# Expert weights read as one 16 KB run per partition, with strided transposes to match

## The reference

```python
def _moe(h, w_router, router_bias, w_gate, w_up, w_down):
    hf = h.reshape(-1, shp[-1])
    combine = _route(hf, w_router, router_bias).astype(h.dtype)
    y = jnp.zeros_like(hf)
    for e in range(N_EXPERTS):
        a = jax.nn.silu(hf @ w_gate[e]) * (hf @ w_up[e])
        y = y + combine[:, e:e + 1] * (a @ w_down[e])
```

## Time and profile before

| | us |
|---|---|
| median of 3 runs | 1851.9 |
| profiled execution, its own time | 1853.53 |
| its span, first to last instruction | 1851.9 |
| mean granted TensorE clock (share of full) | 0.952 |
| PE busy | 1625.3 (88%) |
| DMA queue of SP: 160256 packets, 327.17 MB | 49.4% of 16 engines |
| DMA queue of POOL: 17136 packets, 66.13 MB | 9.5% of 16 engines |

### The profile page before, as it was taken

The page is one execution under the profiler, slowest core; times in us unless marked ns, Lnnn a source line. Parts: engine busy times, 40 slices in busy tenths (PEclk is TensorE's granted clock), DMA queues, the critical chain, the costliest instruction groups (busy, mean ns, idle before and its releaser), DMA issues. The chain is left out here.

```text
span 1851.9 us, 16016 instructions
## 1 busy us (share of the span) xinstructions
PE 1625.3 (88%) x6163; PEld 743.8 (40%) x6163; DVE 481.4 (26%) x1230; ACT 339.5 (18%) x759; POOL 131.6 (7%) x219
## 2 busy tenths in 40 slices
PE   4799998789999999699999969998899939987771
PEld 0244445554444445144444414445444424432220
DVE  1432027850011123301101155117501230011003
ACT  1011027760000021001110112027500111010000
POOL 0100000010000000300000020000200010001001
PEclk9899999999999998899999989999999959998886
DMA  9972232010303044999999996342333177999993
GB/s 345 384 244 91 46 126 119 22 51 32 131 6 136 0 149 160 388 394 365 388 393 393 391 378 206 93 136 97 99 118 113 48 293 273 326 369 387 377 393 110
DMA packets 178194, 396.74 MB, mean 214 GB/s; under 512 B 23694, under 2 KB 27822, under 8 KB 177928
## 3 DMA queue, kind: packets, MB, share of 16 engines
q1 hardware_dynamic: 160256, 327.17, 49.4%
q0 software_dynamic: 17136, 66.13, 9.5%
q10 hardware_dynamic: 724, 2.38, 0.3%
HBM read 373.27 MB, written 34.18 MB: 220 GB/s over the span
## 5 line engine op out<-in xcount | busy, mean ns | idle before, releaser
L1425 PE MATMUL bank<-ring_sb,HT_sb 128*128 128x512 f32 x672 | 296.0, 596 | 4.1 <-ACT HT_sb L703 1.5
L1490 PE MATMUL bank<-ring_sb,HT_sb 128*128 128x512 f32 x576 | 253.3, 592 | 1.4 <-ACT QR_sb L794 1.4
L1425 PEld LDWEIGHTS bank<-ring_sb,HT_sb 128*128 128x128 f32 x672 | 125.8, 191 | 151.2 <-issue 147.6
L1605 PE MATMUL bank<-ring_sb,QR_sb 128*64 128x512 f32 x608 | 148.2, 644 | 41.1 <-DMA ring_sb<-w_e_up 41.1
L1490 PEld LDWEIGHTS bank<-ring_sb,HT_sb 128*128 128x128 f32 x576 | 109.3, 190 | 138.7 <-issue 136.8
L1494 PE MATMUL bank<-ring_sb,QR_sb 128*128 128x512 f32 x288 | 129.5, 592 | 0.0
L1374 PE MATMUL bank<-ring_sb,cT_sb 128*2 128x512 f32 x384 | 95.9, 651 | 31.1 <-DMA ring_sb<-w_mod 30.3
L1591 PE MATMUL bank<-ring_sb,QR_sb 128*128 128x512 f32 x208 | 98.4, 629 | 3.4 <-ACT QR_sb L840 3.4
L1466 PE MATMUL bank<-WK_sb,KR_sb 128*64 128x128 f32 x960 | 68.3, 280 | 36.3 <-ACT WK_sb L804 35.5
L1605 PEld LDWEIGHTS bank<-ring_sb,QR_sb 128*64 128x64 f32 x608 | 49.2, 148 | 126.3 <-issue 126.2
L1621 PE MATMUL bank<-ring_sb,QR_sb 128*128 128x512 f32 x208 | 91.8, 594 | 0.0
(11 more groups left out here) (214 smaller groups left out, 1361.7 us busy)
## 6 DMA issues: line engine op xcount, KB each, us to landing
ring_sb<-w_e_gate SPq DMA_DIRECT2D x32, 2048.0 KB, 19.0
ring_sb<-w_e_up SPq DMA_DIRECT2D x32, 2048.0 KB, 21.4
ring_sb<-w_e_down SPq DMA_DIRECT2D x32, 2048.0 KB, 21.5
ring_sb<-w_mod SPq DMA_DIRECT2D x24, 2048.0 KB, 16.3
ring_sb<-w_in SPq DMA_DIRECT2D x22, 2048.0 KB, 17.3
MB_sb<-mod_d POOLq DMA_DIRECT2D x16, 512.0 KB, 8.7
ring_sb<-w_branch SPq DMA_DIRECT2D x8, 1024.0 KB, 10.0
ring_sb<-w_out SPq DMA_DIRECT2D x4, 2048.0 KB, 10.3
```

What stands on the lines that cost most here:

```text
L1425: ins = mm(bank[j % 4][:, :], HT[:, k, P * t:P * t + P], WR[slot][:, k], start=(k == 0), stop=(k == KD - 1))
L1490: ins = mm(bank[i % 2][:, :], HT[:, k, P * t:P * t + P], WR[wg][:, k], start=(k == 0), stop=(k == KD - 1))
L1605: ins = mm(bank[0][HALF * side:HALF * side + HALF, :], hgT[q % 2][:, k, 0:HALF], WR[slot][:, k], start=(k == 0), stop=(k == KD - 1))
```

## The change

The weight loads take a different row order: partition p now gets rows p*8 to p*8+7 of gate and up (p*4 to p*4+3 of down), which lie one after the other in DRAM, 16 KB for each partition. Before it got rows p, p + 128, p + 256, ..., in runs of 2 KB (gate, up) or 4 KB (down). Block k of the weights therefore holds the rows p*8 + k, so block k of the transposed rows must hold the channels p*8 + k: the transposes read their stationary operand with a step of 8 elements (rows) or 4 elements (hidden values). Neither the number of instructions nor their order changes, nor any wait. All other weights (`w_mod`, `w_in`, `w_branch`, `w_out`) keep their loads, and the rows, stores and gathers of POOL too. The last two hunks of the diff lie in a path that runs only when an expert gets more tokens than it has rows.

```diff
             def expert_source(l, e, j):
                 w = t_in[("w_e_gate", "w_e_up", "w_e_down")[j]]
                 w = w[l, e] if isinstance(e, int) else w[l, bass.ds(e, 1)].rearrange("o k n -> (o k) n")
-                return w.rearrange("(k p) n -> p k n", p=P)
+                return w.rearrange("(p k) n -> p k n", p=P)
...
-                def rows_of(src, q, dst, count):
-                    if full_rows(l, q):
-                        return transposes(src, dst, count)
+                def spread(src, rows, dst, count, first=0, parts=None):
+
+                    by_k = src.rearrange("q (p k) -> q k p", k=parts or count)
                     for k in range(count):
-                        ins = mm(dst[:, HALF * k:HALF * k + HALF], src[0:HALF, P * k:P * k + P],
-                                 ident[0:HALF, 0:HALF], start=True, stop=True, is_transpose=True)
+                        ins = mm(dst[:, rows * k:rows * k + rows], by_k[0:rows, first + k], ident[0:rows, 0:rows],
+                                 start=True, stop=True, is_transpose=True)
                     return ins
...
                     if full_rows(l, q):
                         for g in range(2):
-                            ins = transposes(hg[q % 2][:, CW * g:CW * g + CW], bank[6 + g], 4)
+                            ins = spread(hg[q % 2], P, bank[6 + g], 4, 4 * g, KD)
                     else:
-                        ins = rows_of(hg[q % 2], q, bank[6], KD)
+                        ins = spread(hg[q % 2], HALF, bank[6], KD)
                     ins.then_inc(hg_tr, 1)
...
-                    rows_of(ea, q, bank[2], 4).then_inc(ea_tr, 1)
+                    spread(ea, P if full_rows(l, q) else HALF, bank[2], 4).then_inc(ea_tr, 1)
```

More of the change, by code:

```diff
@@ L1664, in _ @@
                         for g in range(2):
-                            ins = transposes(hg[0][:, CW * g:CW * g + CW], bank[6 + g], 4)
+                            ins = spread(hg[0], P, bank[6 + g], 4, 4 * g, KD)
                         ins.then_inc(q["hg_tr"], 1)
@@ L1673, in _ @@
                         eng.wait_ge(q["a"], n + 1)
-                        transposes(ea, bank[3], 4).then_inc(q["a_tr"], 1)
+                        spread(ea, P, bank[3], 4).then_inc(q["a_tr"], 1)
                         eng.wait_ge(q["aT"], n + 1)
```

## The result

| | us |
|---|---|
| before, median of 6 runs | 1854.51 (1851.51 to 1856.8) |
| after, median of 6 runs | 1863.47 (1859.33 to 1867.74) |
| ratio | 1.005, 95% interval 1.0038 to 1.0063 |
| profiled execution of after, own time and span | 1859.33 and 1857.7 |

The change makes the kernel 0.5% slower, about 9 us (1863.47 less 1854.51). The profiled execution of after is the fastest of its six; its span is 5.8 us longer than that of before, and only these 5.8 us can be followed in the trace.

A forecast was written before the change was run, and what follows sets the result against it. PE was taken to bound layer 0, weight loads layer 1's last nine experts, with each stage's start a third place. -12.8 - 1.8 + 13.6 + 4.6 = +3.6 us on 1851.9 gave about 1855 us, range 1838 to 1869.

The forecast's parts named there:

- Gain in layer 1: Layer 1's last nine experts, bound by weight loads: faster long runs save 12.8 us (10 to 19).
- The start of layer 0: SP's 16 KB runs delay POOL's scatters and row load before layer 0's first transposes: +13.6 us (0 to +17).
- The rival without starving: Layer 0's start: scatters are not delayed by long runs, so the +13.6 falls away: 1842 us; chance 0.25.
- Eight periods: Layer 1's tail, 1656.81 to 1798.12 us: 1.22 us saved per expert, 9.8 us in all (8.8 to 13.6).
- Ahead of expert 7: Layer 1, loads queued before expert 7's 5.15 us wait: 2.3 us by run prices, 3 us taken.
- The waits and the stride in layer 0: Two 0.9 us weight waits vanish (-1.8); strided transposes cost 0.2 us an expert, +4.6 over 23 experts of both layers.
- Strided loads twice as long: Transposes of 23 experts: weight loads 140 ns longer each, up to 39 us, 1890 us at most; chance 0.17.
- one sign of being wrong: Expert transposes: taking 1.5 times as long would show the forecast wrong.
- The end of layer 0: Modulation loads come sooner, but row store, gather and DVE hold the step: 0 us, low end -3.
- Runs that do not merge: SP's queue: runs stay 2 and 4 KB, only the stride is left, 1852 to 1866 us; chance 0.08.
- slower reads: Weight loads in both layers: long runs read 5% slower, +7 us and +13 us, 1877 us with stride; chance 0.05.
- strides of which half hides: Transposes: half of the doubled weight-load time stays hidden, giving 1872 us; case within a rival of chance 0.17.

The follow-up runs named there:

- the short early runs: After, but the weight loads of experts 0 and 1 go as two DMAs of even and odd blocks, in 2 and 4 KB runs: 1846.23 us, ratio 0.9962.
- the spread row loads: After, with layer 1's half-expert rows on 128 partitions in 2 KB runs (1850.57 us, ratio 0.9983) or on even partitions in 4 KB runs (1851.79 us, ratio 0.9983).
- VectorE's order: After with plain transposes: VectorE writes normalised rows and hidden values in block order, and router weights are loaded in that order: 1855.4 us, ratio 1.0015.
- the two kernels with short early runs: After with 2 and 4 KB runs for experts 0 and 1: 1846.23 us; the same with VectorE writing in block order and plain transposes: 1841.03 us.
- the stride alone: After's row order and strided transposes, but every load as two DMAs of even and odd blocks, so runs stay 2 and 4 KB: 1858.2 us, ratio 1.0033.
- the last kernel: After with short runs for experts 0 and 1, VectorE's block order, and both layers' half-expert rows spread over 128 partitions, four transposes replacing eight: 1829.38 us, ratio 0.9867.
- both repairs: After with short runs for experts 0 and 1, and plain transposes with VectorE writing in block order: 1841.03 us, ratio 0.9934.

## Why the prediction came out as it did

The time lies in the range, on the side of the forecast's sign (+3.6), but 8.5 us above the likeliest value, and as slower where "within 0.3%" was thought likelier. Of the 8.5 us, 2.6 are the kernel before, whose median of six is 1854.51 us where that of three was 1851.9. That it lies in the range is partly luck: the largest gain of the sum was 5 us too large, and only the width of the range took that in. The step that failed is the one headed "Gain in layer 1".

- **The start of layer 0** was forecast at +13.6 us and is +13.2. The row load goes out at 785.20 us instead of "near 787", after a wait of 30.61 us, and its rows start the first transposes 3.8 us later (3.9 forecast), at 789.00 for 791. One run for one run, whatever its length, holds from 2 to 16 KB as a share, and the short early runs took the delay away. The rival without starving is refuted.
- **Eight periods**, "8 x 1.22 = 9.8 us", gave 7.3. The price of the runs was right: with the rows spread out, before has 17.32 us and after 15.92 to 15.96, 1.4 apart (1.22 forecast, 1.7 its high end), and 1.4 less the difference of 0.5 is the 0.9 a period that was won. What the term left out is that POOL's row loads onto partitions 0 to 63 stretch the weight runs beside them, and those of 16 KB by more: 1.0 us a period against 0.5. So the forecast of a "new period" of 16.4 us came out at 16.75 over all eight. The term took POOL's part of a period to be the same before and after.
- **Ahead of expert 7** I took 3 us and got 0.2. The wait itself fell by 1.9 us (5.15 to 3.21, "under 3" was forecast), but nearly all of that is PE coming later: its work in the three stretches between half experts' products ahead of that wait grew by 0.6 us each, and the weights came only 0.2 us sooner. That they could have come sooner is shown by the spread row loads: in the two kernels that differ from after only in them, the wait vanishes and the stretch takes 128.14 and 128.90 us instead of 131.47 (130.15 to 131.78 in the other kernels with long runs and rows on partitions 0 to 63). With "Eight periods" this is the miss: 12.8 us forecast, 7.7 measured.
- **The waits and the stride in layer 0.** The prediction has -1.8 us for the waits and +4.6 for the stride, of which 3.2 (16 experts at 0.2) fall on layer 0: +1.4. The stage lost 1.9 us. That sum came out by luck of three parts. The stride costs 5.3 us: 4.9 (after against VectorE's order) or 4.3 (the two kernels with short early runs, 289.45 and 285.11 us), and 5.3 from either pair when the first gate product, which follows PE's long wait at a reduced clock, is left out. Of it 4.3 lie on the seven half experts (0.61 each, the high bound of the prediction), the rest on the nine full ones, where I had spread 0.2 us over each. Against it stand the two waits (-1.8), which the stride alone takes away as well, and the first gate product (-1.4: 10.04 us to the start of the next one at a granted clock of 0.69 in before, 8.61 us at 0.81 in after). That product takes 8.4 to 9.6 us in all other kernels here, whatever their runs, so the 1.4 is no gain of the change.
- **Strided loads twice as long.** By the prediction's rival the loads would be twice as long; they are 1.42 times as long (202 against 140 ns and less), far from doubled. That is the direction of the rule of the Trainium skill (SBUF — State Buffer, Specifications (TRN2)) weighed there, and not the size of a halved read rate. But one sign of being wrong that the prediction named, "transposes that take 1.5 times as long", did come for half experts (1.09 against 0.71 us, 0.69 against 0.46): the cover that the 0.2 us relied on is there only with 128 moving columns.
- **The end of layer 0** was put at 0 and is 0 (-0.2 over the whole stretch).
- **Runs that do not merge, and slower reads** did not come: 2677 runs of 16 KB in seven periods, and at 615 ns, with the row loads spread out, they are as fast as the 0.61 estimated. Two figures of the rivals were summed wrongly: slower reads leave out the start's +13.6 us and would give about 1890 us, not 1877, and strides of which half hides give 1870, not 1872.
- **From trace to median.** The account above explains 5.7 us; the medians are 9 apart. The profiled execution of after ran at a mean clock of 0.953 and was the fastest of six, the five others at 0.948 to 0.951. The 1.6 us by which PE reaches the stage earlier and the 1.4 of the first gate product, neither of which comes from the change, are as large as the missing 3 us. That they are it was not tried.

## What to carry to other kernels

- Before longer DMA runs go into one queue, look for small transfers of another queue that share its time and that an engine waits for. By the counts here they get one run through for each of the long ones; keep runs short exactly there (here two experts of sixteen), and look at what stands behind them in the queue before you hold loads back instead.
- A transfer onto half of the partitions can slow the big loads beside it. Where DMA is the bound, spread small row loads over partitions of both halves, even at the price of more runs. Here the even partitions alone took 12 us off after and 4.5 off before; in the last kernel, on top of longer runs and both repairs (0.7%), the spread rows with their fewer transposes were worth another 0.7%.
- Put a stride on the engine with time to spare: VectorE's 0.37 us an operation cost PE 0.3 us in a stage and up to 1.4 us ahead of each router, TensorE's 60 ns a weight load cost 5 us in layer 0, four fifths of it where the moving side was too short to hide it.

## What was not expected of the hardware

- Row loads onto partitions 0 to 63 make 16 KB runs of the other queue take 654 instead of 615 ns on average and cut the rate from 428 to 401 GB/s; the same bytes on even partitions do not.
- A TensorE weight load of float32 with a step of 4 or 8 elements takes 198 to 202 ns instead of 138 to 140 (both steps are in each mean); a VectorE write with a step of 512 bytes takes 1.06 us instead of 0.69 for 512 values.
- Two queues shared the engines by the number of runs, not by bytes: 284 to 281 with 16 KB against 4 KB. Seven stores of 4 KB took 20.54 us of wait beside four 2 MB loads of 16 KB runs.
